# Another order of loads and splits at the start of a two-block transformer kernel

## The reference

```python
def rms_norm(x, g):
    xf = x.astype(jnp.float32)
    y = xf * lax.rsqrt(jnp.mean(xf * xf, axis=-1, keepdims=True) + NORM_EPS)
    return (y * g.astype(jnp.float32)).astype(x.dtype)

def first_block(x, p, positions, w_in, ...):
    h = x
    for i in range(DEPTH):                       # DEPTH = 2
        u = rms_norm(h, norm_g[i])
        z = u @ w_in[i]                          # 2048 x 7176 weights
        ...                                      # three attention mixers, rotary angles from positions
        h = h + mixed @ w_o[i]
        h = h + (p[i] @ w_ple[i]) * jax.nn.sigmoid(h @ w_pg[i])
    return rms_norm(h, final_g)

def reference(x, ...):
    x = first_block(x, ...)
    return second_block(x, ...)                  # retention, mLSTM, a PEER layer
```

## Time and profile before

| what | us |
|---|---|
| median of 3 runs | 3915.91 |
| lowest and highest of them | 3911.89, 3919.79 |
| the profiled execution's own time | 3924.32 |
| its span in the profile | 3922.7 |
| TensorE busy in the span | 3765.9 (96%) |
| VectorE, ScalarE busy | 2353.0 (60%), 1550.2 (40%) |

### The profile page before, as it was taken

One profiled execution on the slowest core, in us unless ns is written; L12 is line 12 of the kernel. 1 busy time (PEld: TensorE's weight loads), 2 busy tenths in 40 slices (PEclk: granted clock), 3 DMA queues, 4 the chain that ended last, 5 costly groups with the idle time before them and its releaser, 6 DMA issues.

```text
span 3922.7 us, 49916 instructions
## 1 busy us (share of the span) xinstructions
PE 3765.9 (96%) x21042; PEld 3208.2 (82%) x21042; DVE 2353.0 (60%) x3127; ACT 1550.2 (40%) x1518; POOL 101.3 (3%) x145
## 2 busy tenths in 40 slices
PE   8999999999999679999999989999999999999998
PEld 6777777777777468887888889999999999988886
DVE  3455644436554367656665569867655665567777
ACT  3344534333444331135543333345533333333333
POOL 0000000000000000010000000000000000000000
PEclk8999999999999889999999999999999999999999
DMA  5545565645555537643356535556666666666664
GB/s 202 199 166 199 195 232 192 249 161 184 203 214 207 185 140 284 240 146 134 133 200 243 208 140 182 193 193 240 234 221 217 228 218 225 224 232 246 230 242 172
DMA packets 117959, 799.31 MB, mean 204 GB/s; under 512 B 13136, under 2 KB 13520, under 8 KB 29456
## 3 DMA queue, kind: packets, MB, share of 16 engines
q1 hardware_dynamic: 96704, 692.73, 48.9%
q0 software_dynamic: 18768, 82.96, 5.7%
q10 hardware_dynamic: 2304, 20.97, 1.3%
HBM read 752.57 MB, written 44.04 MB: 203 GB/s over the span
## 4 chain that ended last, share of the span: by engine, by line
PE 56%; DVE 5%; DMA 1%; ACT 1%; issue 1%; DVEq 0%; ACTq 0%; POOLq 0%; POOL 0%; SPq 0%
PE ps L293 17%; PE ps L295 17%; PE ps L294 17%; DVE ring_r L307 2%; PE ps L1678 1%; DMA ring<-in_stream_dram 1%; PE ps L1537 1%; DVE z L3139 0%; DVE act L2903 0%; PE ps L1486 0%; PE ps L1500 0%; DVE z L3135 0%; PE ps L1414 0%; ACT high L301 0%; PE ps L1658 0%
## 5 line engine op out<-in xcount | busy, mean ns | idle before, releaser
L301 ACT CAST high<-ring 128x2048 fp32r<-128x2048 f32 x384 | 733.9, 1912 | 1303.4 <-DMA ring<-in_stream_dram 1298.3
L307 DVE TENSOR_TENSOR ring_r<-ring,high 128x2048 fp32r<-128x2048 f32 x384 | 878.8, 2290 | 550.4 <-ACT high L301 545.4
L295 PE MATMUL ps<-high,act_r 128*128 128x512 f32 x1888 | 743.5, 394 | 0.0
L293 PE MATMUL ps<-high,z_r 128*128 128x512 f32 x1856 | 733.1, 395 | 1.8 <-DVE z L3257 1.6
L294 PE MATMUL ps<-ring_r,z_r 128*128 128x512 f32 x1856 | 727.0, 392 | 0.0
L294 PE MATMUL ps<-act_r,high 128*128 128x256 f32 x2496 | 707.8, 284 | 0.0
L293 PE MATMUL ps<-act_r,high 128*128 128x256 f32 x2304 | 656.9, 285 | 10.2 <-DVE ring_r L307 9.8
L295 PE MATMUL ps<-act_r,ring_r 128*128 128x256 f32 x2304 | 652.7, 283 | 0.0
L293 PE MATMUL ps<-high,h_r 128*128 128x512 f32 x1472 | 599.5, 407 | 47.3 <-DVE ring_r L2314 23.8
L2314 DVE TENSOR_TENSOR ring_r<-ring,high 128x2048 fp32r<-128x2048 f32 x176 | 401.5, 2288 | 306.7 <-ACT high L1786 304.9
L294 PE MATMUL ps<-ring_r,h_r 128*128 128x512 f32 x1472 | 580.4, 394 | 0.0
(11 more groups left out here) (474 smaller groups left out, 3157.5 us busy)
## 6 DMA issues: line engine op xcount, KB each, us to landing
ring<-in_stream_dram SPq DMA_DIRECT2D x656, 1024.0 KB, 4.8
hidden<-z POOLq DMA_DIRECT2D x32, 512.0 KB, 3.8
gate_matrix<-z ACTq DMA_DIRECT2D x8, 2048.0 KB, 6.3
r<-gate_matrix POOLq DMA_DIRECT2D x32, 512.0 KB, 6.7
z<-hidden POOLq DMA_DIRECT2D x32, 512.0 KB, 7.2
r<-in_w_ple_dram POOLq DMA_DIRECT2D x2, 2048.0 KB, 9.5
merge_gates<-r ACTq DMA_DIRECT2D x8, 512.0 KB, 5.4
r<-merge_gates POOLq DMA_DIRECT2D x4, 1024.0 KB, 5.8
```

The source lines that it names most:

```text
L293: pe.matmul(out, lhs[0], rhs[0], start=start, stop=False)
L295: return pe.matmul(out, lhs[1], rhs[0], start=False, stop=stop)
L301: sc.copy(high[:, j, :], ring[:, j, :]).then_inc(piece_high[j], 1)
L307: dve.tensor_tensor(ring_r[:, j, :], ring[:, j, :], high[:, j, :], ALU.subtract).then_inc(piece_low[j], 1)
```

## The change

SyncE now issues two small inputs, the first quarter of x, the first weight piece, the second quarter, the second piece, and so on up to the fourth piece, then the positions, frequencies, lambdas and `bc`. TensorE turns the first quarter, makes the products of slot 0, turns the second quarter, makes the products of slot 1, and so on; quarter 3 is turned ahead of slot 3. The banks are 4 and 5, for the second quarter 2 and 3. ScalarE and VectorE split a quarter and a piece by turns; ScalarE's squares, sines and exponential stand behind the roundings of quarter 3 and ahead of the cast of the fourth piece, VectorE's angles behind the low parts of quarter 3, and its factors in slot 7. What is computed is the same.

```diff
@@ -571,6 +571,7 @@
+        X_BANKS = ((4, 5), (2, 3), (4, 5), (4, 5))
@@ -914,19 +915,24 @@
+            def load_x(e):
+                sp.dma_start(hx[:, :, e * CHUNK:(e + 1) * CHUNK], t["x"][:, e * CHUNK:(e + 1) * CHUNK].rearrange("(t p) d -> p t d", p=P))\
+                  .then_inc(x_loaded[e], 16)
+
             sp.dma_start(cols[:, :], t["cols"]).then_inc(consts, 16)
             sp.dma_start(wsmall[:, 0:256], t["wtail"]).then_inc(consts, 16)
-            sp.dma_start(bc[:, :], t["bc"].partition_broadcast(P)).then_inc(consts, 16)
-            sp.dma_start(sti[:, 0:NT], t["positions"]).then_inc(small, 16)
-            sp.dma_start(zs[:, 0:32], t["inv_freq"].partition_broadcast(P)).then_inc(small, 16)
-            sp.dma_start(zs[:, 512:1024], t["lam"].partition_broadcast(P)).then_inc(small, 16)
-            for e in range(4):
-                sp.dma_start(hx[:, :, e * CHUNK:(e + 1) * CHUNK], t["x"][:, e * CHUNK:(e + 1) * CHUNK].rearrange("(t p) d -> p t d", p=P))\
-                  .then_inc(x_loaded[e], 16)
-            for c, j, b, u in RING:
+            load_x(0)
+            for i, (c, j, b, u) in enumerate(RING):
                 if u >= 1:
                     sp.wait_ge(piece_used[b], u)
                 sp.dma_start(ring[:, b, :], t["stream"][c, j]).then_inc(piece_full[b], 16)
+                if i < 3:
+                    load_x(i + 1)
+                elif i == 3:
+                    sp.dma_start(sti[:, 0:NT], t["positions"]).then_inc(small, 16)
+                    sp.dma_start(zs[:, 0:32], t["inv_freq"].partition_broadcast(P)).then_inc(small, 16)
+                    sp.dma_start(zs[:, 512:1024], t["lam"].partition_broadcast(P)).then_inc(small, 16)
+                    sp.dma_start(bc[:, :], t["bc"].partition_broadcast(P)).then_inc(small, 16)
@@ -1368,11 +1374,18 @@
-                    for e in range(4):
+                    def turn_first(e):
+
                         pe.wait_ge(x_loaded[e], 16)
-                        turn_x(e, (2 * e, 2 * e + 1))
+                        if e >= 2:
+                            pe.wait_ge(tile_low, TILES(0, "x", 4 * e - 6))
+                        turn_x(e, X_BANKS[e])
+
+                    turn_first(0)
                     for l in range(DEPTH):
                         for q in range(SLOTS):
+                            if l == 0 and q in (1, 2, 3):
+                                turn_first(q)
                             for p, blocks in parts_of(q):
                                 products(l, p, blocks)
@@ -1987,21 +2000,22 @@
-                    sc.wait_ge(consts, 16 * 3)
+                    sc.wait_ge(consts, 16 * 2)
                     sc.activation(cols[:, C_SILU:C_SILU + 2 * KT], cols[:, C_SILU:C_SILU + 2 * KT], ACT.Silu)
+                    for e in range(3):
+                        round_x(0, e, X_BANKS[e])
+                        split(0, e)
+                        if e == 0:
+                            sc.copy(tail_high, wtail[:, 0]).then_inc(tail_made, 1)
+                    round_x(0, 3, X_BANKS[3])
+                    for e in range(4):
+                        sc.wait_ge(x_loaded[e], 16)
+                        square_x(hx, e)
+                    sc.drain().then_inc(x_square, 1)
                     sc.wait_ge(trig_made, 1)
...
-                    for e in range(4):
-                        round_x(0, e, (2 * e, 2 * e + 1))
-                    sc.copy(tail_high, wtail[:, 0]).then_inc(tail_made, 1)
-                    for q in range(3):
-                        split(0, q)
-                    for e in range(4):
-                        sc.wait_ge(x_loaded[e], 16)
-                        square_x(hx, e)
-                    sc.drain().then_inc(x_square, 1)
@@ -2541,6 +2555,8 @@
+                        if l == 0 and q == 7:
+                            lam_factors()
@@ -2648,11 +2664,29 @@
-                    dve.wait_ge(small, 16 * 3)
+                    dve.wait_ge(consts, 16 * 2)
+                    for e in range(3):
+                        split_x(0, e, X_BANKS[e])
+                        if e == 0:
+                            dve.wait_ge(tail_made, 1)
+                            dve.tensor_tensor(tail_low, wtail[:, 0], tail_high, ALU.subtract).then_inc(tail_made, 1)
+                        split(0, e)
+                    split_x(0, 3, X_BANKS[3])
+                    dve.wait_ge(small, 16 * 4)
@@ -2684,20 +2718,6 @@
-                    dve.wait_ge(consts, 16 * 3)
-                    for e in range(4):
-                        split_x(0, e, (2 * e, 2 * e + 1))
-                    dve.wait_ge(tail_made, 1)
-                    dve.tensor_tensor(tail_low, wtail[:, 0], tail_high, ALU.subtract).then_inc(tail_made, 1)
-                    for q in range(3):
-                        split(0, q)
...
```

More of the change, by code:

```diff
@@ L2649, in side, with lam_factors @@
                                 ada_dve(dve, ADA_LAYER * l + a0)
+                    def lam_factors():
+                        dve.wait_ge(lam_exp, 1)
+                        e = st[:, 64:68].rearrange("p (l k) -> p l k", k=2)
+                        chain(dve, "dve", dve.tensor_tensor(st[:, 60:62], e[:, :, 1], e[:, :, 0], ALU.subtract))
+                        for ly in range(DEPTH):
+                            init = 0.8 - 0.6 * float(np.exp(-0.3 * ly))
+                            dve.tensor_scalar(st[:, 60 + ly:61 + ly], st[:, 60 + ly:61 + ly], -init, None, ALU.add)
+                            dve.tensor_scalar(bc[:, B_SUB + ly * HD:][:, 0:HD], bc[:, B_SUB + ly * HD:][:, 0:HD], 1.0 - init, None, ALU.mult)
                     dve.memset(mod_rows, 0.0)
```

## The result

| | us |
|---|---|
| kernel before, median of 4 runs | 3917.85 (3911.89 to 3920.51) |
| changed kernel, median of 4 runs | 3944.26 (3941.70 to 3947.73) |
| ratio, 95% interval | 1.0071, 1.0057 to 1.0085 |
| profiled executions, own time, before and after | 3924.32 and 3941.7 |
| their spans | 3922.7 and 3940.1 |

The changed kernel is slower by 26 us, 0.7%. Two later executions took 5458 us (kernel before) and 14010 us (experiment 4) at granted clocks of 0.64 and 0.44, and stand in no comparison here.

What follows compares the result with a forecast made beforehand. TensorE bounds the kernel (56% of the chain), through the fourth piece's start: 15.0 + 3 x 15.35 + 7.0 + 7.0 + 15.0 = 90.1 us, giving 3957; less 7 for clock, 3950, taken as 3948 us; range 3931 to 3960.

Steps and rivals of the forecast that it cites:

- head start: TensorE's first product, with x and the first piece loaded earlier: at 15.0 us instead of 23.5, gain 8.5 us.
- three gaps: TensorE before pieces 1, 2 and the fourth: transposes, roundings, cast, subtraction in series, 7.0, 7.0 and 15.0 us.
- half clock: TensorE's clock falls in each gap; pieces take 15.35 us instead of 8.23, with 7.1 us given back for one piece.
- Full clock throughout: Case of the sum: all first pieces at 8.23 us, gaps 6.6, 6.6 and 14.6, fourth piece at 67.5 us, +7.0 us.
- No slack: Behind the fourth piece's start, all is tied to TensorE's progress, so the kernel's end moves by as much.
- the sum: Start of the fourth piece from first product, three pieces and three gaps; cases +32.5, +7.0 and +18.6 us.
- not slower: Rival: TensorE at full clock from its first product, squares not delaying the fourth piece; 3923 us; chance 0.07 with anything like it.
- half clock throughout: Rival: TensorE's first pieces all at half clock, fourth piece at 90.1 us, time 3957 us; chance 0.18.
- early full clock: Rival: TensorE's clock returns early in the first pieces, 3943 us, down to 3931 if gaps cost none; chance 0.15.
- third gap: TensorE's wait before the fourth piece, with ScalarE's squares (6.2 us) and sines and exponential (1.8 us): 15.0 us.
- The loads do not come early: Rival at the start: each transfer as late as now, first product at 18 us, 3 us on top of any case.

Runs made afterwards that it cites:

- experiment 4: Kernel before with only the loads changed, quarters of x and weight pieces by turns behind the small inputs, compute as before: 3924.9 us, ratio 1.0025 to kernel before.
- experiment 1: Changed kernel with TensorE turning each quarter of x one slot earlier: 3916.78 us, ratio 1.0009 to the kernel before.
- experiment 2: Changed kernel with squares, sines, exponential and angles moved behind the splits of slots 3, 4 and 5: 3938.54 us, ratio 1.0052 to the kernel before.
- experiment 5: Changed kernel with TensorE kept busy where it waited, by transposes of the identity that nobody reads: 3928.55 us, ratio 1.0036 to the kernel before.
- Experiment 6: Kernel before with 80 transposes of the identity filling TensorE's 8.8 us wait for the first split: 3911.05 us, ratio 0.9993 to the kernel before.
- experiment 8: Changed kernel, turning one slot ahead, squares behind splits of slots 3 to 5, 28 filling transposes before slot 0: 3898.34 us, ratio 0.9961; again 3904.18 us, 0.9969.
- experiment 3: Changed kernel with turning one slot ahead and the squares behind the splits of slots 3 to 5: 3906.14 us, ratio 0.9981 to the kernel before.

## Why the prediction was right

It said 3948 us, 32 above the median of before; measured are 3944.3 and 26. The mechanism stands: head start, three gaps behind transposes, and half clock. The sizes of the first two are right; that of the third is partly luck.

1. **Head start.** Predicted 15.0 us for the first product, 8.5 gained; measured 14.11 and 9.35. The first quarter landed 4.5 us after its issue, not 5.6, and the piece at 9.3 us, not 10.0. Issued earlier, with fewer transfers ahead, they were also quicker in this execution.
2. **Gaps.** Predicted 7.0, 7.0 and 15.0 us at half clock, 6.6 and 14.6 at full; measured 7.11 at half, and 6.52 and 14.34 with the transposes at full clock. Experiments 1 and 2 take the causes away one by one, and the waits go with them: the place of the transposes for the first two, the squares and sines for 7.9 us of the third.
3. **Full clock throughout.** Predicted 67.5 us for the fourth piece; experiment 5 has 66.3. The old order at full clock would be 23.5 + 3 x 8.23 = 48.2; experiment 6 has 48.31.
4. **Half clock.** The forecast gave back 7.1 us, what one piece loses at half clock; in the profiled run the three pieces took 38.5 us, 7.5 less than three at half. Its 3948 us put the fourth piece at about 84 us; it came at 80.59. That this came out so well is partly luck, since it varies from run to run. The rule of the clock falling in each gap held for the second and third; before slot 1 the clock was at half already. I also read the column wrongly where it says 1.00 until 19.2 us in the kernel before: its first transposes are 0.21 us apart, and 0.11 us only from 12.3 us on, so the clock was at half until then. The fourth piece lost 1.9 us to half clock, not 2.9.
5. **No slack.** True up to 344 us (shift 21.9 us), and in all twelve profiled runs to about 3 us. The step that I did not have is that later stretches of half clock differ between two executions, 3.3 us in this pair, so that a difference of two profiled executions is not the sum of the start alone.
6. **The base.** I set the sum against the profiled execution and then came down towards the median because its start had been unusually slow. Experiment 6 supports that: removing the half clock altogether from that start brings about 4 us in the median (its interval includes none), though it cost 12 us in the profiled run. All cases of the sum, the 3923 us of "not slower" too, were reckoned from that execution with its late start; against the median of before, that rival's 3923 us would be 7 us slower.

The rivals: half clock throughout (3957) and early full clock (3943, down to 3931) bracket the result; 3944 us lies at the edge of the second. Since the three pieces in the profiled run stood at half clock for some 30 of their 38.5 us, the forecast's mechanism fits better, but by the time alone the two are not told apart. "Not slower" falls: both of its conditions, full clock and squares out of the third gap, were missing; with them and the transposes moved (experiment 8) the change is faster than before by 0.3 to 0.4%. "The loads do not come early" falls with the first product at 14.11 us.

## What to carry to other kernels

When work is cut into steps so that a product can start early, the preparation of step n+1 must stand ahead of the product of step n on the engine that does both; put behind it, every engine waits for the other at each step, here for 28 us against a head start of 9. Look at the busy time of the helpers inside the product's stretches: 0.00 there is the sign, and moving the transposes one step ahead, with the squares three splits later, made the same idea faster than the kernel it came from, if only by 0.2%. A side task without a reader belongs behind the next preparation on its engine, not in front of it.

## What the runs showed of the hardware

- In these traces the granted clock reads 1.00 from the span's start until its first fall, whatever it is: piece 0 of the changed kernel took 15.35 us under "1.00", as at 0.50, and 8.2 us in experiment 5 under the same number.
- Transposes against the identity hold and raise TensorE's clock: 80 of them kept the full clock through the old wait (pieces of 8.2 us from the first on), 28 together with sixteen of x brought it up before 14.3 us.
- With wide products and 8-column products by turns, a half clock lasted, from the first product, anything from 2.9 us (experiment 1) and 7.4 us (experiment 3) to 26.6 us (kernel before), while a full clock held for three pieces (experiment 6). With wide products alone it rose after 3.6 us (fourth piece of the changed kernel) to 4.4 us (that of experiment 2). With the small ones 24 at a time it fell behind two of the three lots.
- The first quarter of x landed 5.6 us after its issue in the kernel before, with 0.6 MB ahead of it. With 0.2 MB ahead and the same loads behind, it took 4.5 us (changed kernel) to 5.3 us (experiment 1), so most of the difference in one pair can be chance.
